# An RWKV layer's bonus sums: next to the output product, or between the gate tiles with the value product on GpSimd in the chunk loop

## What is computed

```python
r, k, v, decay, a = to_heads(r), to_heads(k), to_heads(v), to_heads(decay), to_heads(a)
k = k * (1.0 + (a - 1.0) * k_a.astype(F32))
_, y = lax.scan(step, S0, xs)            # the recurrence over the sequence
y = head_norm(y, ln_g, ln_b, RW_GN_EPS)
y = y + jnp.sum(r * k * r_k.astype(F32), axis=-1, keepdims=True) * v     # the bonus
y = y.reshape(B, T, RW_WIDTH) * jax.nn.silu(g.astype(F32))
return y.astype(h.dtype) @ w_out
```

## Time and profile before

| | us |
|---|---|
| median of 3 runs | 1472.85 |
| lowest and highest run | 1472.31, 1475.32 |
| the profiled execution | 1473.26 |
| its span, from first to last instruction | 1471.2 |
| PE busy in it | 1356.5 (92%) |
| DVE busy | 719.3 (49%) |
| ACT busy | 440.6 (30%) |
| POOL busy | 90.7 (6%) |
| mean granted TensorE clock | 0.98 |

### The profile page before, as it was taken

One profiled execution on the slowest core, in us unless ns is written; L12 is line 12 of the kernel. 1 busy time (PEld: TensorE's weight loads), 2 busy tenths in 40 slices (PEclk: granted clock), 3 DMA queues, 4 the chain that ended last, 5 costly groups with the idle time before them and its releaser, 6 DMA issues. The chain is left out here.

```text
span 1471.2 us, 23885 instructions
## 1 busy us (share of the span) xinstructions
PE 1356.5 (92%) x10291; PEld 713.6 (49%) x10291; DVE 719.3 (49%) x1388; ACT 440.6 (30%) x964; POOL 90.7 (6%) x82
## 2 busy tenths in 40 slices
PE   5999999988798999889899989898999999988897
PEld 3444444487544444464444446544444444478633
DVE  5784656855643002261344023434684755955552
ACT  1114243277401011460112052501114253177501
POOL 0000240100000000000000000000000241000000
PEclk9999999999999999999999989998999999999989
DMA  6222222001400222101222221113222222101211
GB/s 208 72 72 56 61 70 62 25 4 61 176 0 1 73 84 72 58 2 57 74 71 72 72 56 29 57 57 113 80 72 57 72 59 69 32 4 61 75 58 57
DMA packets 111184, 92.47 MB, mean 63 GB/s; under 512 B 5020, under 2 KB 99524, under 8 KB 110568
## 3 DMA queue, kind: packets, MB, share of 16 engines
q1 hardware_dynamic: 110376, 88.81, 19.9%
q10 hardware_dynamic: 704, 2.13, 0.4%
HBM read 84.64 MB, written 6.29 MB: 62 GB/s over the span
## 5 line engine op out<-in xcount | busy, mean ns | idle before, releaser
L893 PE MATMUL bank<-arena 128*128 128x512 f32 x960 | 420.1, 594 | 1.5 <-ACT arena L541 1.5
L893 PEld LDWEIGHTS bank<-arena 128*128 128x128 f32 x960 | 180.6, 190 | 224.9 <-issue 219.1
L848 PE MATMUL bank<-arena 64*64 64x64 f32 (+2 forms) x6720 | 187.6, 225 | 29.8 <-ACT arena L599 8.9
L848 PEld LDWEIGHTS bank<-arena 64*64 64x64 f32 (+1 forms) x6720 | 164.5, 135 | 66.0 <-issue 37.5
L1215 PE MATMUL bank<-arena 128*128 128x512 f32 x256 | 116.9, 618 | 4.7 <-DVE arena L1180 4.7
L159 ACT ACTIVATE arena<-arena 128x1024 f32<-128x1024 f32 x20 | 21.1, 1055 | 244.6 <-DVE arena L1186 133.4
L1215 PEld LDWEIGHTS bank<-arena 128*128 128x128 f32 x256 | 50.2, 198 | 71.8 <-issue 64.7
L1679 PE MATMUL bank<-arena 128*128 128x512 f32 x160 | 71.0, 605 | 1.6 <-PEq L301 1.6
L653 DVE SCALAR_TENSOR_TENSOR arena<-arena 128x512 f32<-128x512 f32 x96 | 72.2, 802 | 0.0
L495 POOL MEMSET arena<- 128x8 f32 x2 | 0.2, 113 | 932.9 <-DVE arena L808 932.9
L1311 PE MATMUL bank<-arena 128*128 128x512 f32 x128 | 55.2, 593 | 1.6 <-PEq L1124 1.6
(11 more groups left out here) (233 smaller groups left out, 1652.3 us busy)
## 6 DMA issues: line engine op xcount, KB each, us to landing
arena<-in_rw_w_in SPq DMA_DIRECT2D x66, 512.0 KB, 4.1
arena<-in_ml_w_in SPq DMA_DIRECT2D x24, 512.0 KB, 3.8
arena<-in_sw_w_in SPq DMA_DIRECT2D x20, 512.0 KB, 3.7
arena<-in_rw_w_out SPq DMA_DIRECT2D x16, 512.0 KB, 7.1
spill<-arena SPq DMA_DIRECT2D x2, 2048.0 KB, 8.4
arena<-spill SPq DMA_DIRECT2D x2, 2048.0 KB, 8.5
arena<-in_sw_w_out SPq DMA_DIRECT2D x8, 512.0 KB, 3.7
arena<-in_ml_w_out SPq DMA_DIRECT2D x8, 512.0 KB, 3.7
```

The lines of the kernel that those rows point to most:

```text
L848: mm = lambda out, a, b, start=True, stop=True: nc.tensor.matmul(out, a, b, start=start, stop=stop, skip_group_check=True)
L893: last = nc.tensor.matmul(bank[:, :], slot[:, k, :], mix_at[what][:, k, :], start=k == 0, stop=k == KT - 1)
```

## The change

The bonus matmuls move to `rw_mix`, two behind each of the first four gate tiles, into banks 0 to 3, which are free there once all A products are evacuated. ACT copies each sum from its bank over the tile of R (`keep_bonus`). In the chunk loop POOL multiplies one tile of R by one tile of V for each chunk, ahead of the square of that chunk's outputs. In `rw_gate_out` the matmuls, DVE's products, their semaphores and the waits on these banks go, L1178 reads the finished bonus from R, and the final norm's weights go to the room of V without a wait.

```diff
+BONUS_AT = {0: (0, 1), 1: (2, 3), 2: (4, 5), 3: (6, 7)}
...
+            pool.wait_ge(t_turned.handle, t_turned.at(1))
             for c in range(NC):
+
+                pool.wait_ge(bonus_kept.handle, bonus_kept.at(c + 1))
+                nc.gpsimd.tensor_tensor(R[:, c, :], R[:, c, :], V[:, c, :], ALU.mult)
...
+            def keep_bonus(j):
+                act.wait_ge(bonus_done.handle, bonus_done.at(j + 1))
+                nc.scalar.activation(R[:, j, :], bonus_bank(j)[:, :], ACT.Copy).then_inc(bonus_kept.handle, 1)
...
             for j in range(KT - 1):
                 read_tile(place["g", j])
+                for i in BONUS_AT.get(j, ()):
+                    keep_bonus(i)
...
+            def bonus(j):
+                if j == 0:
+                    pe.wait_ge(ga_evac.handle, ga_evac.at(2 * NC))
+                    pe.wait_ge(scaled_rk.handle, scaled_rk.at(NC))
+                if j >= 4:
+                    pe.wait_ge(bonus_kept.handle, bonus_kept.at(j - 3))
+                mm(bonus_bank(j)[:, :], bones, R[:, j, :]).then_inc(bonus_done.handle, 1)
...
-            for n in range(place["g", 0], len(tiles) - 1):
-                project(n)
-            pe.wait_ge(ga_evac.handle, ga_evac.at(2 * NC))
+            for j in range(KT - 1):
+                project(place["g", j])
+                for i in BONUS_AT.get(j, ()):
+                    bonus(i)
+            pe.wait_ge(bonus_kept.handle, bonus_kept.at(KT))
             turn_values(0)
...
-    fg = m.view(B_R, D)
+    fg = m.view(B_V, D)
...
-                sp.wait_ge(bonus_done.handle, bonus_done.at(KT))
...
-            for j in range(6):
-                add_bonus(j)
-
             dve.wait_ge(root.handle, root.at(1))
             nc.vector.reciprocal(rstd, rstd).then_inc(inverse.handle, 1)
-            for j in range(6, KT):
-                add_bonus(j)
...
-            for j in range(4):
-                bonus(j)
             pe.wait_ge(ready.handle, ready.at(1))
...
-            for j in range(4, KT):
-                bonus(j)
-
```

More of the change, by code:

```diff
@@ L465, in rw_mix @@
     s_cleared, scaled_rk = m.sem("s_cleared"), m.sem("scaled_rk")
+    bonus_done, bonus_kept = m.sem("bonus_done"), m.sem("bonus_kept")
+    bonus_bank = lambda j: m.bank[j % 4]
     gathered, step, t_turned, tu_cleared, t_placed, u_placed = (m.sem(n) for n in (
@@ L1089, in rw_mix @@
                  (gr_evac, 2 * NC), (bkt_done, 2 * NC), (bkt_evac, 2 * NC), (gathered, 1), (step, steps[0]), (t_turned, 1),
-                 (tu_cleared, BC), (s_cleared, 1), (scaled_rk, NC), (t_placed, NC), (u_placed, NC)):
+                 (tu_cleared, BC), (s_cleared, 1), (scaled_rk, NC), (bonus_done, KT), (bonus_kept, KT), (t_placed, NC), (u_placed, NC)):
         s.base += n
@@ L1102, in rw_gate_out @@
     nc = m.nc
-    R, V, G, Y, sq = (m.view(b, KT, T) for b in (B_R, B_V, B_G, B_KK, B_L))
+    bonus, G, Y, sq = (m.view(b, KT, T) for b in (B_R, B_G, B_KK, B_L))
     W = m.view(B_K, KT, D)
@@ L1106, in rw_gate_out @@
     rstd = m.view(A_DX, T)
-    bones = m.view(A_CONST + C_BONES, P)
     compact = lambda i: m.view(A_CONST + C_COMPACT + 14 - 2 * i, 4)
     group = lambda j: slice(32 * (j % 4), 32 * (j % 4) + 4)
-    fg = m.view(B_R, D)
+    fg = m.view(B_V, D)
     eps = m.view(A_SMALL + 40, 1)
@@ L1115, in rw_gate_out @@
         "var_bank_ready", "var_done", "root_ready", "rstd_ready", "pick_loaded"))
-    bonus_done, bonus_used, spread_done, spread_used, finished, out_done, chain = (m.sem(n) for n in (
-        "bonus_done", "bonus_used", "spread_done", "spread_used", "y_finished", "out_done", "dve_chain"))
+    spread_done, spread_used, finished, out_done, chain = (m.sem(n) for n in (
+        "spread_done", "spread_used", "y_finished", "out_done", "dve_chain"))
     w_loaded = [m.sem(f"w_out{k}_loaded") for k in range(KT)]
     spread_bank = lambda j: m.bank[(0, 7, 5, 6)[j % 4]]
-    bonus_bank = lambda j: m.bank[1 + j % 4]
     added, fg_loaded, stored = m.sem("h_added"), m.sem("final_g_loaded"), m.sem("stored")
@@ L1155, in link @@
                 dve.wait_ge(chain.handle, chain.at(links[0]))
-            def add_bonus(j):
-                dve.wait_ge(bonus_done.handle, bonus_done.at(j + 1))
-                nc.vector.tensor_tensor(V[:, j, :], bonus_bank(j)[:, :], V[:, j, :], ALU.mult).then_inc(bonus_used.handle, 1)
             nc.vector.memset(eps, 64e-5)
             nc.vector.memset(m.bank[0][:, :], 1.0).then_inc(ready.handle, 1)
-            for j in range(6):
-                add_bonus(j)
             dve.wait_ge(root.handle, root.at(1))
             nc.vector.reciprocal(rstd, rstd).then_inc(inverse.handle, 1)
-            for j in range(6, KT):
-                add_bonus(j)
             for j in range(KT):
@@ L1176, in _ @@
                 dve.wait_ge(spread_used.handle, spread_used.at(j + 1))
-                dve.wait_ge(bonus_used.handle, bonus_used.at(j + 1))
-                link(nc.vector.scalar_tensor_tensor(out=Y[:, j, :], in0=Y[:, j, :], scalar=col(RW_LNB, j), in1=V[:, j, :],
+                link(nc.vector.scalar_tensor_tensor(out=Y[:, j, :], in0=Y[:, j, :], scalar=col(RW_LNB, j), in1=bonus[:, j, :],
                                                     op0=ALU.add, op1=ALU.add))
@@ L1206, in spread @@
                                      start=True, stop=True).then_inc(spread_done.handle, 1)
[L1208 to L1211, removed]
             def out_product(half, a, k):
@@ L1236, in _ @@
                 for a in range(NT):
-                    if k == 0:
-                        pe.wait_ge(bonus_used.handle, bonus_used.at(a + 5))
                     last = out_product(0, a, k)
@@ L1251, in _ @@
                     norm.turn(pe, a)
-    for s, n in ((ready, 1), (var_done, 1), (root, 1), (inverse, 1), (pick_loaded, 64), (bonus_done, KT), (bonus_used, KT),
+    for s, n in ((ready, 1), (var_done, 1), (root, 1), (inverse, 1), (pick_loaded, 64),
                  (spread_done, KT), (spread_used, KT), (finished, KT), (out_done, 8), (added, 8), (chain, links[0])):
```

## The result

The changed kernel is slower.

| | before, median us | changed, median us | ratio, 95% interval |
|---|---|---|---|
| first set, 4 runs each | 1474.09 | 1483.76 | 1.0060 (1.0044 to 1.0076) |
| second set, 5 runs of the changed, 9 of before | 1473.69 | 1483.82 | 1.0064 (1.0050 to 1.0078) |

What follows compares the result with a forecast made beforehand. PE was taken to bound both the gate stage and the output stage's head: 2 x 6.87 us of bare matmuls less 8.34 us from the heads gives +5.4 us, forecast 1478.2 us, range 1473.5 to 1483.

Steps and rivals of the forecast that it cites:

- What bounds the gate stage: Gate stage: PE is dense and sets its end, so the eight added matmuls cost their whole length, 6.87 us per layer.
- ACT's copies and POOL's products at nothing: Gate stage and chunk loop: eight ACT copies fit in idle time and POOL's products do not delay DVE; cost 0.
- The head's chain: Output stage: spread starts 6.85 us into the block, first output product at 11.27 with the spread at the lower clock.
- The idle time at the block's start: Output stage: PE's idle time before the variance matmuls grows from 1.69 to 2.4 us; the forecast took no clock fall there.
- rival 3: Start of the output block: clock falls early, variance matmuls take 3.8 instead of 1.9 us; 1482.0 us, chance 0.08.
- The gain of the heads: Output stage, block's start to first output product: 3.69 us shorter in the first layer, 4.65 in the last, 8.34 together.
- rival 1: Output stage: clock stays high, gaining 10.24 us in the heads and 2.65 behind each first product; 1471.1 us, chance 0.08.
- The half rate behind the first output product: Output stage: the 5.3 us at half rate behind the first output product's start were left as they are.
- the forecast's own mechanism: Gate stage pays for all bonus matmuls, shorter heads give part back; 1475.5 to 1481 us by spread clocks, chance 0.70.

Runs made afterwards that it cites:

- e1_extra: The kernel before with eight more bonus-shaped matmuls in each RWKV layer's gate stage, results unread; 1489.37 us against 1475.18, ratio 1.0109.
- e3_no_pool: The changed kernel without POOL's sixteen products in the chunk loop; 1483.89 us, ratio 1.0064 to the kernel before.
- e6_before_filled: The kernel before with two filler matmuls behind the last bonus matmul and two behind the spread, per layer; 1468.45 us against 1475.34, ratio 0.9955.
- c1_under_root: The kernel before with the bonus matmuls kept in the output stage but moved into PE's idle time there; 1460.70 us against 1475.34, ratio 0.9902.
- e2_no_sums: The changed kernel without the gate stage's bonus matmuls and ACT's copies; 1470.76 us against 1475.18 for the kernel before, ratio 0.9972.
- e4_pe_busy: The changed kernel with seven filler matmuls in the head of each output stage; 1475.89 us against 1475.18 for the kernel before, ratio 1.0007.
- e5: The changed kernel with one filler matmul ahead of each layer's variance matmuls; 1480.10 us against 1475.34 for the kernel before, ratio 1.0036.

## Why the prediction was right, and where it was short

The direction and the mechanism were right; the size was short by 3.5 to 4 us of 8.9 to 9.4.

- *What bounds the gate stage.* Right: no matmul was hidden, 6.87 us per layer in both the changed kernel and e1_extra.
- *ACT's copies and POOL's products at nothing.* Right, both by the rows and by e3_no_pool. DVE's L775 was not held longer.
- *The head's chain.* Right to 0.02 us in the first layer, with the spread at the lower clock in both, as taken.
- *The idle time at the block's start.* This step failed. The prediction named a clock that falls before the variance matmuls as rival 3, gave it 0.08, and priced it at 1.9 us per layer. It came in six of eight profiled heads, and cost 0.95 us per head on average (12.2 instead of 11.27). The gain of the heads is thus 30.88 − 24.4 = 6.4 us, not 8.34. The prediction gives no row against this rival, and it held a row for it: under rival 1 it says that 2.3 us of idle time were already followed by a fall in both layers, and the 2.4 us here are no shorter.
- *The half rate behind the first output product.* Left as it was, and nearly right: its first sixteen records took 9.50 us on average of the eight heads, against 9.79 and 9.88 before, 0.7 us in all.
- *What is left.* 13.7 − 6.4 − 0.7 = +6.6 us is what the two stages explain. The measured +8.9 and +9.4 have intervals that reach down to 6.5 and 7.4, so 6.6 lies at the edge of the one and outside the other. The profiled executions also differ in stages that the change does not touch, and two such places can be named; as far as ten profiled executions show, neither is the change's.

The first is in the attention layer's projection stage, which took 2.1 us more in the changed kernel (474.69 to 620.24) than in the kernel before (471.73 to 615.20). Windows of PE just behind the stage's start, in this order in the kernel before, the changed one and e6_before_filled, where it starts at 469.94:

```profile
476.00:477.00 1.00, 1.00 (x4) 1.00 0.05 0
476.00:477.00 1.00, 1.00 (x2) 0.50 0.04 0
470.00:471.00 1.00, 1.00 (x2) 0.50 0.00 0
```

The granted clock is at half rate there in eight of the ten profiled executions, e1_extra, e6_before_filled and c1_under_root among them; only those of the kernel before and of e2_no_sums have it high. The program of this stage is the same in all ten, so as far as one execution of each tells, the change does not make this difference.

The second is in the chunk loop, which with the block's end took 97.04 us in the first layer before and 95.62 and 99.38 in two executions of the changed kernel. In 16 of the 20 loops profiled, with either place of the bonus, the third distance between POOL's squares is 12.4 to 16.6 us instead of 12.05. PE waits there for nothing that the profile shows; in the kernel before:

```profile
339.07 3.40 PE L848 MATMUL bank<-arena 64*64 64x64 f32 x104 [1.14 <-issue]
```

This explains how single executions of one kernel come to differ by several microseconds. Why the medians keep some 2 us more than the two stages give stays open. e2_no_sums has a gap as well: its profiled execution took 1466.31 us, 6.95 less than that of the kernel before, as its heads and the records behind them say (7.2), but the median of its twelve runs gains only 4.1 to 4.4. For e1_extra the median agrees (14.2 for 13.7) and the ratio is 2 us high. So these runs don't tell which half the 2 us belong to.

The predicted 1478.2 us was 5.6 us low in absolute time, and the upper end of the range, 1483.0, fell 0.8 us short of both medians. Part of this is the base: the runs known before had a median of 1472.85, the later ones of 1473.69 to 1475.34; on 1472.85 the measured +8.9 us would give 1481.7. That is inside the range, but above the 1475.5 to 1481 of the forecast's own mechanism and next to the 1482.0 of rival 3. So the direction came from the sum, but the size that was measured needs a rival that was given 0.08, and some 2 us that nobody had in the sum. Rival 1, a clock that holds, did not come by itself, but e4_pe_busy and e6_before_filled show that its price, 2.65 us per layer, was right.

## What to carry to other kernels

A matmul that lies on the critical path in one stage is not free in another because other engines idle there: look whether PE itself has a gap, and put the work into PE's own idle time. In this kernel such gaps stood right beside the work, under a square root and a reciprocal, and filling them paid twice, once for the work and once for the clock that no longer fell. When an edit shortens a chain by taking PE's work out of it, price the half rate that the longer idle time can bring.

## What the runs showed of the hardware

Idle stretches of 2.4 us ahead of the variance matmuls were followed, in six of eight profiled heads, by a fall of the granted clock to half within them; with 1.69 us and a matmul of 128x512 ahead of them, it fell in none of the twelve heads of before, e1, e4, e5, e6 and c1. These are single profiled executions of each kernel, and what PE did in the loop before is the same in all of them. Useless matmuls made a kernel faster: eight of them in e6_before_filled save 0.45%. When a DVE product with both inputs in the arena waits for a POOL instruction and a second POOL instruction is queued behind it, DVE goes first and the POOL instruction is stretched (1.46 us against 1.04), so in this loop back-to-back work on POOL delayed DVE by the one running instruction only.
